# Where the last two attention units, the first expert list and the second block's chain stand

## What is computed

```python
def peer(h, w_q, subkeys, u, v):            # per chunk of 128 tokens, xc (128, 1024)
    q = (xc @ w_q).reshape(C, 8, 2, 128)
    s = jnp.einsum('chpd,hpnd->chpn', q, subkeys)          # key sums, 2 x 128 for each head
    sv, si = lax.top_k(s, 16)
    cand = sv[:, :, 0, :, None] + sv[:, :, 1, None, :]     # 256 candidates
    best, pos = lax.top_k(cand.reshape(C, 8, 256), 16)     # 16 of them, and their ids
    g = jax.nn.softmax(best, axis=-1)
    ue, ve = jnp.take(u, ids, axis=0), jnp.take(v, ids, axis=0)
    a = jax.nn.gelu(jnp.einsum('cd,chkd->chk', xc, ue))
    return jnp.einsum('chk,chkd->cd', g * a, ve)
...
x = x + g1x * attention(norm1(x)) @ w_out                  # before it
x = x + g2x * peer(norm2(x) * (1 + sc2x) + sh2x)
```

## Time and profile before

| | us |
|---|---|
| median of three runs | 1515.83 (1513.65 to 1516.47) |
| the profiled execution, its time | 1516.59 |
| its span, first to last instruction | 1514.8 |
| PE busy | 1340.8 (89%) |
| DVE busy | 1073.6 (71%) |
| ACT busy | 604.4 (40%) |
| POOL busy | 276.6 (18%) |

### The profile page before, as it was taken

The page is one execution under the profiler, slowest core; times in us unless marked ns, Lnnn a source line. Parts: engine busy times, 40 slices in busy tenths (PEclk is TensorE's granted clock), DMA queues, the critical chain, the costliest instruction groups (busy, mean ns, idle before and its releaser), DMA issues.

```text
span 1514.8 us, 18538 instructions
## 1 busy us (share of the span) xinstructions
PE 1340.8 (89%) x6164; PEld 920.1 (61%) x6164; DVE 1073.6 (71%) x2244; ACT 604.4 (40%) x1227; POOL 276.6 (18%) x263
## 2 busy tenths in 40 slices
PE   7998897879797978979797798998999999899998
PEld 2786653634343534434343345778999876799987
DVE  4598845576777767676777757977887478788864
ACT  5343632232222121222222214565665355656652
POOL 0000003254334444434334430000000000000000
PEclk9999999989899998989899899999999999999999
DMA  9624435889999999999999996434455344344540
GB/s 396 244 111 157 177 135 203 358 342 421 421 421 422 421 422 422 422 422 422 422 421 422 421 422 255 167 122 157 168 194 194 128 154 167 112 168 173 195 161 29
DMA packets 49845, 416.19 MB, mean 275 GB/s; under 512 B 5488, under 2 KB 5616, under 8 KB 7024
## 3 DMA queue, kind: packets, MB, share of 16 engines
q0 software_dynamic: 36864, 268.45, 42.8%
q1 hardware_dynamic: 12912, 146.82, 25.4%
HBM read 414.20 MB, written 1.05 MB: 274 GB/s over the span
## 4 chain that ended last, share of the span: by engine, by line
PE 50%; DVE 16%; DMA 15%; issue 10%; POOL 6%; ACT 3%; POOLq 0%; DVEq 0%; ACTq 0%; SPq 0%
DMA arena<-in_uv,ids 15%; PE ps L1078 6%; PE ps L1333 6%; PE ps L1332 6%; PE ps L1331 6%; PE ps L1145 4%; PE ps L1147 4%; PE ps L1146 4%; POOL arena L733 3%; POOL ring L733 3%; DVE ring L2011 2%; PE ps L864 2%; PE ps L865 2%; PE ps L866 2%; PE ps L934 1%
## 5 line engine op out<-in xcount | busy, mean ns | idle before, releaser
L1078 PE MATMUL ps<-ring,arena 128*128 128x512 f32 x512 | 257.1, 666 | 99.6 <-ACT arena L1539 99.6
L1078 PEld LDWEIGHTS ps<-ring,arena 128*128 128x128 f32 x512 | 108.0, 214 | 243.4 <-issue 132.9
L2011 DVE CUSTOM_DVE_ANT_0 arena<-arena 128x1024 f32<-128x1024 f32 x128 | 156.8, 1226 | 131.2 <-DMA arena<-in_uv,ids 131.1
L564 DVE TENSOR_TENSOR arena_r<-ring,arena_r 128x1024 fp32r<-128x1024 f32 x152 | 185.0, 1223 | 58.0 <-ACT arena_r L549 57.6
L1078 PE MATMUL ps<-arena 128*128 128x512 f32 x512 | 223.7, 594 | 0.0
L1331 PE MATMUL ps<-hH,arena_r 128*128 128x256 f32 x704 | 199.5, 283 | 0.0
L1333 PE MATMUL ps<-hH,arena_r 128*128 128x256 f32 x704 | 199.4, 283 | 0.0
L1332 PE MATMUL ps<-arena_r 128*128 128x256 f32 x704 | 199.4, 283 | 0.0
L733 POOL DMA_INDIRECT ring<-in_uv,ids x128 | 143.5, 1121 | 279.7 <-PE ps L1078 228.7
L733 POOL DMA_INDIRECT arena<-in_uv,ids x128 | 132.5, 1035 | 331.5 <-issue 258.9
L549 ACT ACTIVATE arena_r<-ring 128x1024 fp32r<-128x1024 f32 x152 | 158.9, 1053 | 58.9 <-PE ps L1147 58.6
(11 more groups left out here) (300 smaller groups left out, 2001.7 us busy)
## 6 DMA issues: line engine op xcount, KB each, us to landing
ring<-in_lw SPq DMA_DIRECT2D x39, 2048.0 KB, 7.8
ring<-in_b1w SPq DMA_DIRECT2D x18, 2048.0 KB, 8.8
wqb<-in_wq SPq DMA_DIRECT2D x8, 1024.0 KB, 8.9
ring<-in_lw SPq DMA_DIRECT2D x8, 1024.0 KB, 5.1
ring<-in_lw SPq DMA_DIRECT2D x2, 1088.0 KB, 11.4
arena<-in_uv,ids POOLq DMA_INDIRECT x128, 26.6
ring<-in_uv,ids POOLq DMA_INDIRECT x128, 19.4
cst<-in_const SPq DMA_DIRECT2D x1, 1487.5 KB, 19.1
```

Source lines behind the costliest of these rows:

```text
L564: nc.vector.tensor_tensor(low_of(l, p), piece_raw(p), high_of(l, p).bitcast(F32), ALU.subtract)\
L1078: last = nc.tensor.matmul(ps[:, 4 + 2 * c + b, :], diag[:, k % 4, :], vrows[at[k]][:, b * 512:(b + 1) * 512], start=False, stop=(close and ...
L2011: V.tensor_tensor_reduce(out=urows[at], in0=urows[at], in1=hrow[:, c, :], scale=1.0, scalar=0.0, op0=ALU.mult, op1=ALU.add, accum_out=dots ...
```

## The change

It moves instructions. Added are only those that working out the first list in two halves asks for; taken out are two of ACT's table loads, since stage 0's gelus stand together.

- **PE.** The loop over attention units ends with unit 13. All 16 steps of the first block's projection stand by then. The transposition of the second block's heads follows, four steps of its projection (before: eight), and the first block's transposition, queries and key sums. Behind these come `turn` and `values` of units 14 and 15, with four more steps between. `mod_rows` moves behind the second block's projection, and `mod_cols` and the second `mod_rows` behind the second block's key sums. `keys(1)` stands in front of all experts of stage 0, which are no longer cut.
- **PE and its feeders.** `queries` takes its eight inputs in the order 0, 4, 1, 5, 2, 6, 3, 7 and waits for each singly (`n2_act`, `n2_dve` count by tile); before, it waited for all eight.
- **DVE.** `residual` is split, with the probabilities of units 14 and 15 behind its halves. `first_topk` works out the best 8 of 256 and their ids (`first_ids`), then the other 8 (`ids_ready`). The second block's chain and its `topk` come in front of all dots of stage 0 but two.
- **ACT.** The square root's table is loaded in front of the copy of the turned heads (`heads_in(3)`); `act_pt` and `act_rows` of units 14 and 15 stand behind the first block's queries; the second block's root (`roots(1, 6)`) stands behind `mod_row_out`, the copy of `mod_rows`' result; both softmaxes and all of stage 0's `experts` stand behind `query_out(1)`.
- **POOL.** Gather 0 waits for `first_ids` and for `pv_done` 16 (unit 15's values), gather 8 for `ids_ready`. The order of the pairs and their other waits are as before.

```diff
@@ gpsimd
-            pool.wait_ge(ids_ready, 1)
+            pool.wait_ge(first_ids, 1)
...
+                if k == 0:
+                    pool.wait_ge(pv_done, 16)
+                elif k == 8:
+                    pool.wait_ge(ids_ready, 1)
@@ tensor
+            pe.wait_ge(wo_out, 1)
+            turned(1, range(4, KD), 7)
...
             out_sums(0, 2, 0, 1, 2, 3)
-            out_sums(1, 3, 0, 1, 2, 3)
...
+                    for i in range(KD):
+                        k = i // 2 + 4 * (i % 2)
+                        if s == 0:
+                            pe.wait_ge(n2_dve if i % 2 else n2_act, 4 * c + i // 2 + 1)
...
             key_sums(0).then_inc(first_s, 1)
-            pe.wait_ge(wo_out, 2)
+            turn(14)
+            out_sums(1, 3, 0, 1)
+            values(14)
+            turn(15)
+            out_sums(1, 3, 2, 3)
+            values(15)
             back_to_rows(0, (0, 7))
...
             turned(1, range(4), 0)
+            cleared(4, 5)
             pe.wait_ge(o_out, 4)
             out_sums(0, 2, 4, 5, 6, 7)
             out_sums(1, 3, 4, 5, 6, 7)
-            pe.wait_ge(row_out, 2)
-            mod_cols(MOD_A + MOD_B, 7)
-            mod_rows(MOD_A + MOD_B + 1, 6)
+            pe.wait_ge(pv_out, 16)
+            mod_rows(MOD_A + MOD_B, 6)
             norm2_tiles(1, (0, 2))
...
+            pe.wait_ge(row_out, 2)
+            mod_cols(MOD_A + MOD_B, 7)
+            mod_rows(MOD_A + MOD_B + 1, 6)
...
-            experts(0, 0, part=range(4), at=FIRST_SLOTS)
+            pe.wait_ge(row_out, 4)
+            keys(1)
             mod_cols(MOD_A + MOD_B + 1, 3)
+            experts(0, 0, at=FIRST_SLOTS)
             pe.wait_ge(mod_out, MOD_A + MOD_B + 1)
             cleared(6, 7)
-            experts(0, 0, part=range(4, 8), at=FIRST_SLOTS)
-            pe.wait_ge(row_out, 4)
-            keys(1)
-            experts(0, 0, part=range(8, TOPK), at=FIRST_SLOTS)
@@ scalar
+            act_rows(act, 13)
             table(ACT.Sqrt)
+            heads_in(3, range(4, KD), 7)
...
+            mod_row_out(MOD_A + MOD_B, 6)
+            roots(1, 6)
+            norm2_in(1)
+            queries_in(1, 3, q_done, q_out)
+            rows_in(1, (0, 2))
+            mod_row_out(MOD_A + MOD_B + 1, 6)
...
+            query_out(1)
             softmax(0, 0)
-            experts(0, 0, groups=(0,))
-            table(ACT.Sqrt)
...
             softmax(1, 1)
-            experts(0, 0, groups=(2, 3))
+            experts(0, 0)
```

More of the change, by code:

```diff
@@ L944, in _ @@
             scores(1)
-            for m in range(16):
+            for m in range(14):
                 if m + 2 < 16:
@@ L965, in _ @@
                     pe.wait_ge(o_out, 2)
-                    out_sums(0, 7, 0, 1)
+                    out_sums(0, 7, 0, 1, 2, 3)
                 elif m == 13:
-                    out_sums(0, 7, 2, 3)
+                    out_sums(0, 7, 4, 5, 6, 7)
                     pe.wait_ge(mod_out, MOD_A + MOD_B)
[L970 to L979, removed]
+                    out_sums(1, 5, *range(KD))
+            values(13)
+            pe.wait_ge(wo_out, 1)
+            turned(1, range(4, KD), 7)
             pe.wait_ge(exp_done, 32)
@@ L1026, in _ @@
             pe.wait_ge(wq_in, 16)
[L1027 to L1028 removed]
+            pe.wait_ge(wo_out, 2)
+            queries(0, 5).then_inc(first_q, 1)
             pe.wait_ge(sk_in, 16)
@@ L1071, in keys, with experts @@
                 last.then_inc(s_done, 1)
-            def experts(n, c, close=False, part=range(TOPK), at=range(TOPK)):
-                for k in part:
+            def experts(n, c, close=False, at=range(TOPK)):
+                for k in range(TOPK):
                     pe.wait_ge(diag_ready, TOPK * n + k + 1)
@@ L1454, in heads_in, with exponentials @@
                                      ACT.Copy, scale=gain).then_inc(o_out, 1)
-            for m, (c, t) in enumerate(units()):
+            def exponentials(m):
                 act.wait_ge(mx_ready, m + 1)
@@ L1463, in _ @@
                                          accum_out=zs[:, m % 2, s:s + 1]).then_inc(exp_done, 1)
+            for m in range(15):
+                exponentials(m)
                 if m >= 2:
@@ L1527, in softmax, with experts @@
                                      accum_out=pz[:, c, 1:2]).then_inc(prob_done, 1)
-            def experts(n, c, ends=ENDS, groups=None):
-                for g in groups or range(len(ends)):
-                    end, start = ends[g], ends[g - 1] if g else 0
+            def experts(n, c, ends=ENDS):
+                for g, end in enumerate(ends):
+                    start = ends[g - 1] if g else 0
                     act.wait_ge(dots_ready, TOPK * n + end)
@@ L1937, in gated, with residual @@
                     dve.wait_ge(wo_out, call0 + i + 1)
-            def residual(c, banks):
-                for n in range(2):
-                    dve.wait_ge(wo_used, 2 * c + n + 1)
-                    gated(g1b, [(c, n, banks[n])], 2 * c + n)
+            def residual(c, n, bank):
+                dve.wait_ge(wo_used, 2 * c + n + 1)
+                gated(g1b, [(c, n, bank)], 2 * c + n)
             def norm2_rows(c):
@@ L2025, in products @@
                 weights(n, c, len(ends) - 1, ends)
-            topk(0, 0, 0)
+            first_topk()
             heads_variance(1)
             heads_scale(1)
-            dve.wait_ge(row_out, 2)
-            for k in range(4):
-                dot(0, 0, k, FIRST_SLOTS[k])
-            dve.wait_ge(prob_done, 1)
-            run(V.reciprocal(pz[:, 0, 2:3], pz[:, 0, 1:2]))
-            weights(0, 0, 0, ENDS)
-            residual(1, (2, 3))
+            residual(1, 0, 2)
+            residual(1, 1, 3)
             norm2_rows(1)
             norm2_out(1, 2)
+            dve.wait_ge(row_out, 2)
+            for k in range(2):
+                dot(0, 0, k, FIRST_SLOTS[k])
+            topk(1, 0, 1)
             mod_bias(MOD_A + MOD_B, 7)
-            for k in range(4, 8):
+            for k in range(2, TOPK):
                 dot(0, 0, k, FIRST_SLOTS[k])
-            weights(0, 0, 1, ENDS)
-            topk(1, 0, 1)
-            for k in range(8, TOPK):
-                dot(0, 0, k, FIRST_SLOTS[k])
-                if k == 12:
-                    weights(0, 0, 2, ENDS)
+                if k == 3:
+                    dve.wait_ge(prob_done, 1)
+                    run(V.reciprocal(pz[:, 0, 2:3], pz[:, 0, 1:2]))
+                if k % 4 == 0:
+                    weights(0, 0, k // 4 - 1, ENDS)
             weights(0, 0, 3, ENDS)
```

83 lines of the change are left out of this document (49 added, 34 removed).

## The result

The changed kernel takes 1519.0 us in the median of twenty executions (1517.05 to 1523.17), the kernel before, run beside it, 1516.41 (1512.53 to 1519.85). One of the twenty, a slow one of 5446.88 us whose cause is open, is left out of this range and of the ratio. The ratio is 1.0017, 95% interval 1.0009 to 1.0025: **2.6 us slower**, between 1.4 and 3.8. The 2.6 lies under the prediction's bound of 0.2%, 3.0 us; the interval reaches beyond it. The profiled execution took 1519.22 us with a span of 1517.4, against 1516.59 and 1514.8.

A forecast was written before the change was run, and what follows sets the result against it. The unbroken stream of gathers was taken to bound the kernel. A gain of 1.9 us at full clock and 3.5 us for the clock gave +1.6, so 1518.2, or 1517.4 with 0.8 off for the median; range 1511.5 to 1522.

The forecast's parts named there:

- prediction's bound: Whole kernel's time: differences up to about 0.2%, 3.0 us, cannot be told from no change, so 1512.8 to 1518.9 counts as same.
- key sums at DVE: First block's key sums reach DVE at 224.7 us, where it was 230.58 before.
- stage 1's first gather: On POOL's queue, behind the sixth expert: 300.2 us at full clock, by when 18 transfers are over, not 21.
- break-even at 302.1: Start of the unbroken stream: three transfers fewer are over, costing 7.5 us, so it must start by 309.58 - 7.5 = 302.1.
- the stream is not what counts: Rival: PE and DVE bound the stages, so lost transfers cost nothing; 1507 to 1512.8 us, faster, chance 0.12.
- first hole: Stage 0's gathers: the first five transfers end at 248.5, so the DMA engines idle about 5 us before the sixth.
- second hole: Stage 0's gathers of pairs 6, 7 and 13 to 15 wait for the second `mod_rows`: DMA idle from 269 to 278.
- The order on ACT: Second block's root behind the copy of `mod_rows`' result: costs the root 3.7 us, of which PE feels 2.4.
- The table load: In front of the heads' copy on ACT: taken as 1.28 us, without the skill's added drain of about 1.38 us.
- The clock: Half clock on PE behind three idle times: 1.0 + 1.6 + 0.9 = 3.5 us in the mean, bounds 0 and 7.
- three fallen clocks: Rival: the clock falls behind all three PE gaps, one fall lasting long; +4.3 to +5.3, 1520 to 1522 us; slower, chance 0.28.
- trades one late gap for three short ones: PE's idle times on the path: by the skill's clock rule the change is badly placed on a path of PE work.

The follow-up runs named there:

- e2: Changed kernel with stage 1's gathers issued in the order in which buffers come free (FIRST_SLOTS), not 0 to 15; 1509.66 us, ratio 0.9950 to the kernel before.
- e3: Kernel before with only stage 1's gathers reordered to the order in which buffers come free; 1507.58 us, ratio 0.9936 to the kernel before.
- e4: Changed kernel with ACT's second root in front of the copy of `mod_rows`' result instead of behind it; 1515.15 us, ratio 0.9992 to the kernel before.
- e6: Changed kernel with two more products of zeros in each of PE's three gaps of 2.1 to 2.3 us; 1516.1 us, ratio 0.9997 to the kernel before.
- e1: Changed kernel with the first gather waiting for the output projection instead of unit 15's values; 1518.12 us, ratio 1.0012 to the kernel before.
- e5: Changed kernel with `mod_rows` put back into PE's idle stretch, ahead of the second block's heads, ACT's copy likewise; 1513.32 us, ratio 0.9973 to the kernel before.
- e7: Changed kernel with the first expert list worked out in one piece, not in halves; 1517.7 us, ratio 1.0000 to the kernel before.
- e8: Changed kernel with gathers in freeing order, row products in PE's idle stretch, whole first list, zero products in first and third gap; 1502.44 us, ratio 0.9900.

## Why the prediction was right

1517.4 us was forecast, +1.6; measured were 1519.0 and +2.6, within the range, and within the bound of 3.0 us. Of the 1.6 us between 1517.4 and 1519.0, 0.6 is the kernel before, whose median is now 1516.41 and was 1515.83. Step by step:

| step | predicted | trace after |
|---|---|---|
| wait for the turned heads on PE | 2.2 us | 2.21 |
| key sums at DVE | 224.7 | 226.09 |
| first half of the list, from its candidates | 4.0 us | 234.52 - 230.52 = 4.00 |
| second half | 3.9 us | 4.08 |
| first gather | 234.3 | 235.72 |
| sixth gather | 253.1 | 254.06 |
| second block's transposition | 261.7 | 262.54 |
| second `mod_rows` ends | 276.7 | 279.0 |
| first expert | 288.8 | 291.08 |
| stage 1's first gather | 300.2, with 3.5 for the clock 303.7 | 303.90 |

The prediction's own terms give 224.9 for the key sums, not 224.7; nothing hangs on the 0.2 us.

**The bound.** The claim that counts was that the stream of gathers bounds the kernel, with a break-even at 302.1. Stage 1's first gather at 303.90 gives +1.8 by that rule; the span says +2.6. The 0.8 between is less than one pair of executions can tell. The two traces do not start alike either: the last `scores` that stand at the same place in both kernels come 0.45 us later before than after (the lines of before and after below), so with the starts taken off the rule gives +2.2.

```profile
190.28 1.13 PE L888 MATMUL ps<-arena 64*128 64x512 f32 x4
```

```profile
189.83 1.13 PE L892 MATMUL ps<-arena 64*128 64x512 f32 x4
```

The rival "the stream is not what counts" is refuted twice: stage 1's list is there at 281.36, some 9 us earlier than before, and the kernel is slower; and e2 and e3, which change nothing but the order of gathers, gain some 10 us each.

**The halves.** List, sixth gather and first hole are as told: share 0.58 from 248 to 253 us. The second hole is there, but some 3 us later than told. Where the prediction had "near zero", 273 to 277, transfers under way still end, and the engines stand idle from 277 to 281:

```profile
273.00:277.00 4.00, 4.00 (x11) 0.77 (x9) 3.01 (x13) 0.00 (x0) 0.00 (x0) 1.00 0.36 147
277.00:281.00 4.00, 4.00 (x14) 2.04 (x13) 3.50 (x12) 0.59 (x1) 0.94 (x1) 1.00 0.00 0
```

**The order on ACT.** 3.7 us for the root were told, of which PE feels 2.4. The root's input is ready at 256.4 and the root comes at 260.7, 4.3 us; the gap on PE is 2.33, and e4 returns it.

**The table load.** In front of the heads' copy:

```profile
212.04 1.28 ACT L1367 ACT_TABLE_LOAD   x1
213.33 0.20 ACT L1367 ACTIVATE sm<-cst 128x1 f32<-128x1 f32 x1
213.56 0.60 ACT L1457 ACTIVATE arena<-ps 128x512 f32<-128x512 f32 x1
```

The load takes 1.28 us and the next instruction starts 0.01 behind it. The drain of 1.38 us that the Trainium skill adds ("ScalarE: Activation LUTs", "What ACT_TABLE_LOAD costs") is not seen, as the prediction assumed; PE's wait came out at 2.21, without it. Over the whole program ACT has 44 table loads after and 48 before: the change takes out four, not the two that its description gives.

**The clock** was the term of the sum with the wrong size, and the other terms hid it. Against e6's rows the three gaps cost 1.7 + 1.5 + 1.4 = 4.6 us in this execution, where I took 3.5 in the mean, and the steps at full clock were 0.9 us quicker than mine (303.90 - 4.6 = 299.3, for 300.2). That the two nearly cancel, and leave 303.90 where 303.7 was told, is luck; and so in part is the clock's own term, since the first gap costs its 1.7 us in some executions and nothing in others (last section). The rival "three fallen clocks" came true in what it describes, but at 4.6 us and not its 6.2 to 7.2, because transposition and queries lost 1.5 us and not 2.8: I had priced the middle gap from rows 6, where PE waits 1.51 us a second time behind the transposition. Behind one gap of 2.33 us only the first part of the queries ran at half clock (0.50 from 263.4 to 266.7 us, 1.00 from there to 269.0). Where the second wait stands behind a gap of the same 2.33 us, in e3, the queries took 6.48 us.

That the change "trades one late gap for three short ones" does not hold against the prediction's own rows: the kernel before has half clock behind three idle times on the same path, 4.93, 2.15 with 1.51, and 2.76 us (rows 6 and 7). The sum is not touched by this, because the break-even was read from that trace as it ran.

**What the prediction did not see** is that it took the order of stage 1's gathers as given. It noted that pair 0 is the sixth to come free, and computed from it the 300.2; that the wait can be avoided by issuing in the order of freeing, worth about four times the change's effect (10.2 and 9.7 us), it did not ask.

## What to carry to other kernels

Where a stretch is bound by an unbroken stream of transfers, count how many are over when it becomes unbroken; starting it earlier was worth nothing here, because it stopped again, and work on other engines counted through the buffer that it frees for it. Issue refills in the order in which buffers come free, not by index. An idle stretch of an engine is the place for independent work that stands on its path, and short gaps of TensorE are to be merged, filled or avoided: three of about 2.2 us cost 4.6 us here where all three lost the clock, and filling them gave 3.0 us of time back.

## What the runs showed of the hardware

**The same gap does not always cost the clock.** The first gap, 2.21 us in front of the same eight products, stood in six of these kernels unchanged. In two, the changed kernel and e1, the clock fell behind it and the products took 5.37 us; in four (e2, e4, e5, e7) it stayed at full and they took 3.67. e5's line, and its granted clock there, to be read against the changed kernel's 5.37 us at 0.50:

```profile
215.92 3.67 PE L938 MATMUL ps<-ring,arena 128*128 128x512 f32 x8 [2.21 <-issue]
```

```profile
216.00:219.30 3.30, 3.30 (x8) 1.47 (x9) 2.37 (x8) 0.00 (x0) 0.00 (x0) 1.00 0.00 0
```

The third gap, 2.07 to 2.08 us and so shorter, cost the clock in all six (10.27 to 10.55 us for 20 products, 8.85 in e6), the second, 2.33 to 2.40, in all four that have it (5.23 to 5.49 us for 32, 3.92 in e6). So between 2.0 and 2.4 us the length alone does not decide; what else does, these traces do not tell. One profile of such a gap is one draw: here it is worth 1.7 us, more than half of the difference between the two kernels. The timed 2.6 us is taken over executions in which it may fall either way.

**Executions of the same code differ ahead of the edits** by up to 3.5 us at 200 us (198.55 to 202.10), as much as what was to be measured. The granted clock goes with it. The stretches 130 to 150 and 150 to 170 us, in e8, which is the earliest at 200 us, and in e1, the latest:

```profile
130.00:150.00 20.00, 14.63 (x92) 9.78 (x94) 15.85 (x31) 10.77 (x30) 0.00 (x0) 1.00 0.53 214
150.00:170.00 20.00, 17.50 (x120) 12.29 (x116) 16.69 (x32) 12.68 (x36) 0.00 (x0) 1.00 0.60 238
```

```profile
130.00:150.00 20.00, 14.40 (x79) 8.61 (x78) 15.29 (x28) 10.95 (x28) 0.00 (x0) 0.91 0.48 190
150.00:170.00 20.00, 18.13 (x119) 13.24 (x118) 15.46 (x31) 11.66 (x34) 0.00 (x0) 0.91 0.68 270
```

The kernels sort by it. The clock is 1.00 in both stretches in e8, e4 and e2, which reach the place at 198.55 to 199.66; it is 0.91 in one of them in the changed kernel, e6 and e7 (200.26 to 200.95), and in both in e5 and e1 (201.91 and 202.10). The code up to there is the same, so this too changes from one execution to the next. No run changes it on purpose: that the clock makes the difference is read from this order and not shown, and it does not sort the kernels within a group, 1.1 us apart at most.
